# Decoder layer with a product-key expert FFN: three of eight token blocks by gathered rows, gathers two dots early, one-hots scaled on ScalarE

## The reference, cut to what matters

```python
s = jnp.einsum('thpd,hpkd->thpk', q, sub_keys)
s1, i1 = lax.top_k(s[:, :, 0], K); s2, i2 = lax.top_k(s[:, :, 1], K)
cand = (s1[..., :, None] + s2[..., None, :]).reshape(T, H, K * K)
top_s, pos = lax.top_k(cand, K)
idx = jnp.take_along_axis(cand_idx, pos, axis=-1)        # i1 * 128 + i2
g = jax.nn.softmax(top_s, axis=-1)
def block(args):                                          # 128 tokens at a time
    u = jnp.take(u_tab, ib, axis=0)                       # 128 rows of 1024 for each token
    a = jax.nn.gelu(jnp.einsum('cd,ced->ce', xb, u), approximate=False) * gb
    vsel = jnp.take(v_tab, ib, axis=0)
    return jnp.einsum('ce,ced->cd', a, vsel)
```

## Time and profile before

| | us |
|---|---|
| median of 3 runs | 3404.7 (3396.75 to 3407.07) |
| the profiled execution | 3406.95, its span 3405.3 |
| mean granted PE clock of it | 0.951 of 2.4 GHz |
| PE busy | 3045.4 (89%) |
| DVE busy | 2506.8 (74%) |
| POOL busy | 1432.0 (42%) |
| ACT busy | 979.2 (29%) |
| DMA | 695.54 MB, 204 GB/s on average |

### The profile page before, as it was taken

One profiled execution on the slowest core, in us unless ns is written; L12 is line 12 of the kernel. 1 busy time (PEld: TensorE's weight loads), 2 busy tenths in 40 slices (PEclk: granted clock), 3 DMA queues, 4 the chain that ended last, 5 costly groups with the idle time before them and its releaser, 6 DMA issues. The chain is left out here.

```text
span 3405.3 us, 42070 instructions
## 1 busy us (share of the span) xinstructions
PE 3045.4 (89%) x15866; PEld 2729.4 (80%) x15866; DVE 2506.8 (74%) x4479; ACT 979.2 (29%) x1445; POOL 1432.0 (42%) x878
## 2 busy tenths in 40 slices
PE   8996998979998788898888788848999999999997
PEld 6886887869998788898888788847878787878886
DVE  5125773458988877877888776538888888888889
ACT  2113331112222233333333333323333333333331
POOL 4113210006564343343333333336666666656563
PEclk9998999989999998998989899978999999999998
DMA  4214222227775555565555555568787878787882
GB/s 164 99 62 148 91 83 78 76 72 234 247 251 190 184 210 191 203 220 211 178 212 198 188 210 207 212 238 276 278 305 272 294 268 298 273 299 275 281 289 107
DMA packets 294036, 695.54 MB, mean 204 GB/s; under 512 B 20448, under 2 KB 136544, under 8 KB 290656
## 3 DMA queue, kind: packets, MB, share of 16 engines
q1 hardware_dynamic: 190944, 316.66, 28.2%
q0 software_dynamic: 73728, 268.47, 21.8%
q10 hardware_dynamic: 29184, 108.01, 8.2%
HBM read 565.13 MB, written 127.93 MB: 204 GB/s over the span
## 5 line engine op out<-in xcount | busy, mean ns | idle before, releaser
L1066 PE MATMUL z_ps<-hT_hi,u_hi 128*128 128x384 f32 x2048 | 718.6, 351 | 24.1 <-PEq L821 24.1
L794 POOL TENSOR_TENSOR u_lo<-u_raw,u_hi 128x1024 fp32r<-128x1024 f32 x128 | 320.4, 2503 | 994.7 <-ACT u_hi L790 994.5
L1067 PE MATMUL z_ps<-hT_lo,u_hi 128*128 128x384 f32 x2048 | 700.3, 342 | 0.0
L1068 PE MATMUL z_ps<-hT_hi,u_lo 128*128 128x384 f32 x2048 | 698.9, 341 | 0.0
L1357 PE MATMUL y_ps<-v_hi,a_hi 128*128 128x512 f32 x1536 | 603.3, 393 | 65.5 <-DVE a_lo L1458 44.3
L1358 PE MATMUL y_ps<-v_lo,a_hi 128*128 128x512 f32 x1536 | 600.0, 391 | 0.0
L1359 PE MATMUL y_ps<-v_hi,a_lo 128*128 128x512 f32 x1536 | 600.0, 391 | 0.0
L1408 POOL TENSOR_TENSOR v_lo<-room,v_hi 128x1024 fp32r<-128x1024 f32 x128 | 342.2, 2674 | 253.2 <-ACT v_hi L1385 251.5
L1066 PEld LDWEIGHTS z_ps<-hT_hi,u_hi 128*128 128x128 f32 x2048 | 399.3, 195 | 24.7 <-issue 24.2
L1357 PEld LDWEIGHTS y_ps<-v_hi,a_hi 128*128 128x128 f32 x1536 | 289.6, 189 | 139.0 <-DVE a_lo L1458 44.5
L1067 PEld LDWEIGHTS z_ps<-hT_lo,u_hi 128*128 128x128 f32 x2048 | 398.8, 195 | 0.0
(11 more groups left out here) (188 smaller groups left out, 4824.2 us busy)
## 6 DMA issues: line engine op xcount, KB each, us to landing
u_raw<-in_uT SPq DMA_DIRECT2D x128, 512.0 KB
room<-in_v SPq DMA_DIRECT2D x128, 512.0 KB
z<-z_sb ACTq DMA_DIRECT2D x128, 384.0 KB
gates<-g_sb ACTq DMA_DIRECT2D x24, 2048.0 KB
z_in<-z SPq DMA_DIRECT2D x16, 1536.0 KB
g_in<-gates SPq DMA_DIRECT2D x16, 1536.0 KB
room<-z SPq DMA_DIRECT2D x15, 1536.0 KB
room<-gates SPq DMA_DIRECT2D x15, 1536.0 KB
```

Source lines behind the costliest of these rows:

```text
L794: self.nc.gpsimd.tensor_tensor(self.u_lo[e][:], self.u_raw[e][:], self.u_hi[e][:].bitcast(F32), ALU.subtract).then_inc(self.u_lo_in[e], 1)
L1066: nc.tensor.matmul(o, u_hi[e][:, k], hT_hi[:, k, cols], start=(k == 0), stop=False)
L1067: nc.tensor.matmul(o, u_hi[e][:, k], hT_lo[:, k, cols], start=False, stop=False)
L1068: last = nc.tensor.matmul(o, u_lo[e][:, k], hT_hi[:, k, cols], start=False, stop=(k == KT - 1))
```

## The change

Three blocks go by rows and five densely: 384 gathers and dots or additions in each pass where there were 256. z has 640 columns, so the u pass's matmuls have 320 in place of 384, and the v pass has 3840 matmuls in place of 4608. The dots of the u pass are spread unevenly over its turns: 62, 62, 62, 30, 30, 30, 30, 78. Gathers of the u pass are issued two dots ahead of POOL's old place (`EARLY`). The names of the picks are made two heads at a time instead of four. hot1 has two buffers and the multiplication with the gates is four activations with a scale on ACT. h of the third block is loaded once block 0's dots are done.

In the diff SP's program comes first, then PE's, ACT's (`scale_hot` is called in turns from GB on, after z and ahead of `take_gates`), POOL's and DVE's.

```diff
-GB = 2
+GB = 3
-    def names(self, link, half):
+    def names(self, link, two):
-        hs = slice(half * PH // 2, (half + 1) * PH // 2)
+        hs = slice(2 * two, 2 * two + 2)
...
-    RING = 3
-    PER_TURN = GB * PH * TOPK // TB
+    RING, EARLY = 3, 2
+    PER_TURN = [62, 62, 62, 30, 30, 30, 30, 78]
...
+        def own_rows(s, q, n):
+
+            before, k = sum(PER_TURN[:s]), q * 8 + n
+            return range(before + PER_TURN[s] * k // 32, before + PER_TURN[s] * (k + 1) // 32)
...
-                sp.dma_start(h_own[:], d["h"].rearrange("n p c -> p n c")[:, 0:GB]).then_inc(h_here, 16)
+                for b in range(2):
+                    sp.dma_start(h_own[b][:], d["h"][b]).then_inc(h_here[b], 16)
                 for m in range(Q * TB):
+                    done = own_rows(m // Q, m % Q, 0).start // (PH * TOPK)
+                    if done > (own_rows((m - 1) // Q, (m - 1) % Q, 0).start // (PH * TOPK) if m else 0) and done + 1 < GB:
+                        sp.wait_ge(row_used, done * PH * TOPK)
+                        sp.dma_start(h_own[(done + 1) % 2][:], d["h"][done + 1]).then_inc(h_here[(done + 1) % 2], 16)
...
-                    pe.wait_ge(hot_in[g], 4 * gm + n // 2 + 1)
+                    pe.wait_ge(hot_g_in[g], 4 * gm + n // 2 + 1)
...
+                def scale_hot(gm, n):
+
+                    g, t0 = n % 2, gm % Q * GT + 4 * n
+                    act.wait_ge(hot_in[g], 4 * gm + n // 2 + 1)
+                    for t in range(4):
+                        last = nc.scalar.activation(hot1_g[g][:, t], hot1[g][:, t], ACT.Copy,
+                                                    scale=gT[:, t0 + t:t0 + t + 1])
+                    last.then_inc(hot_g_in[g], 1)
...
+                for i in range(EARLY):
+                    gather(i)
...
-                            gather(s * PER_TURN + q * 8 + n)
+                            for i in own_rows(s, q, n):
+                                if i + EARLY < GB * PH * TOPK:
+                                    gather(i + EARLY)
...
-                    elif n == 6 and q % 2:
-                        tk.names(link, q // 2)
+                    elif n == 6:
+                        tk.names(link, q)
...
-                    p = 1 - g
-                    wait(v, hot_in[p], 4 * gm + (n + 1) // 2)
-                    link(nc.vector.tensor_tensor(hot1[:], bc(iota_ps, 1, 4), bc(iT[:, 0, t0:t0 + 4], 2, NK),
-                                                 ALU.is_equal))
-                    nc.vector.tensor_tensor(hot2[g][:], bc(iota_ps, 1, 4), bc(iT[:, 1, t0:t0 + 4], 2, NK), ALU.is_equal)
-                    nc.vector.tensor_tensor(hot1_g[g][:], hot1[:], bc(gT_ps[:, t0:t0 + 4], 2, NK),
-                                            ALU.mult).then_inc(hot_in[g], 1)
+                    for hot, side in ((hot2, 1), (hot1, 0)):
+                        last = nc.vector.tensor_tensor(hot[g][:], bc(iota_ps, 1, 4), bc(iT[:, side, t0:t0 + 4], 2, NK),
+                                                       ALU.is_equal)
+                    last.then_inc(hot_in[g], 1)
...
-                            dot(s * PER_TURN + q * 8 + n)
+                            for i in own_rows(s, q, n):
+                                dot(i)
```

More of the change, by code:

```diff
@@ L711, in __init__ @@
         self.cand, self.cand_left = room.carve(TOPK, TOPK), room.carve(TOPK * TOPK)
-        self.pick = room.carve(2, PH // 2 * TOPK, TOPK)
+        self.pick = room.carve(2, 2 * TOPK, TOPK)
         assert room.taken <= room.LOADED
@@ L716, in __init__ @@
         self.best, self.pos = sb("best", [P, PH, TOPK]), sb("pos", [P, PH, TOPK], U32)
-        self.ab = sb("ab", [P, 2, PH // 2, TOPK], U32)
+        self.ab = sb("ab", [P, 2, 2, TOPK], U32)
         self.gap, self.gap_e = sb("gap", [P, PH, TOPK]), sb("gap_e", [P, PH, TOPK])
@@ L752, in names @@
         link(nc.vector.tensor_tensor(self.pick[:], bc(self.ab[:].rearrange("p a h k -> p a (h k)"), 3, TOPK),
-                                     bc(bc(self.places[:], 1, PH // 2 * TOPK), 1, 2), ALU.is_equal))
+                                     bc(bc(self.places[:], 1, 2 * TOPK), 1, 2), ALU.is_equal))
         for a in range(2):
@@ L969, in _ @@
                 tk.gaps().then_inc(gaps, 1)
-                for half in range(2):
-                    tk.names(link, half)
+                for two in range(PH // 2):
+                    tk.names(link, two)
                 v.wait_ge(exps, 1)
@@ L991, in experts_in @@
         s_in = [sb(f"s_in{j}", [P, 2, NK]) for j in range(2)]
-        iT = sb("iT", [P, 2, P])
+        iT, gT = sb("iT", [P, 2, P]), sb("gT", [P, P])
         hot2 = [sb(f"hot2_{g}", [P, 4, NK]) for g in range(2)]
-        hot1 = sb("hot1", [P, 4, NK])
+        hot1 = [sb(f"hot1_{g}", [P, 4, NK]) for g in range(2)]
         hot1_g = [sb(f"hot1_g{g}", [P, 4, NK]) for g in range(2)]
@@ L997, in experts_in @@
         rows_in = ahead.rows + [sb(f"u_rows{i}", [P, D]) for i in range(RING - len(ahead.rows))]
-        h_own = sb("h_own", [P, GB, D])
+        h_own = [sb(f"h_own{b}", [P, D]) for b in range(2)]
         z_ps = [[bank(f"z_ps{e}{a}") for a in range(2)] for e in range(2)]
@@ L1011, in experts_in @@
         hot_in = [sem(f"hot_in{g}") for g in range(2)]
+        hot_g_in = [sem(f"hot_g_in{g}") for g in range(2)]
         g_done = [sem(f"g_done{g}") for g in range(2)]
@@ L1014, in experts_in @@
         g_stored = [sem(f"g_stored{b}") for b in range(2)]
-        picked_in, h_here = sem("picked_in"), sem("h_own_here")
+        picked_in, h_here = sem("picked_in"), [sem(f"h_own_here{b}") for b in range(2)]
         row_here = [sem(f"u_row_here{i}") for i in range(RING)]
@@ L1141, in _ @@
                             if s >= GB:
+                                scale_hot(gm, n)
                                 if n:
@@ L1184, in _ @@
                 v.wait_ge(const_here, 32)
-                v.wait_ge(h_here, 16)
                 link(nc.vector.tensor_copy(iota_ps, iota[:]))
@@ L1231, in dot @@
                     v.wait_ge(row_here[r], 16 * (i // RING + 1))
+                    if slot == 0:
+                        v.wait_ge(h_here[b % 2], 16 * (b // 2 + 1))
                     wait(v, row_used, i)
-                    nc.vector.tensor_tensor_reduce(rows_in[r][:], rows_in[r][:], h_own[:, b], 1.0, 0.0, ALU.mult, ALU.add,
+                    nc.vector.tensor_tensor_reduce(rows_in[r][:], rows_in[r][:], h_own[b % 2][:], 1.0, 0.0, ALU.mult, ALU.add,
                                                    ahead.z_rows[:, b, slot:slot + 1]).then_inc(row_used, 1)
@@ L1241, in _ @@
                         nc.vector.tensor_copy(iT[:], g_ps[0][:, 0:2])
-                        link(nc.vector.tensor_copy(gT_ps, g_ps[0][:, 2]))
+                        link(nc.vector.tensor_copy(gT[:], g_ps[0][:, 2]))
                     for q in range(Q):
```

## The result

| | before | after |
|---|---|---|
| median (runs) | 3400.7 us (4) | 3594.6 us (4) |
| ratio, with its 95% interval | | 1.057 (1.055 to 1.059) |
| the profiled execution, its span | 3406.95, 3405.3 | 3595.34, 3593.6 |
| mean granted PE clock | 0.951 | 0.885 |

The change makes the kernel 5.7% slower. 3450 us was forecast, with a range of 3310 to 3550.

The account below looks back on a forecast made before the run. PE sets the pace in the v pass and early u turns, DVE close behind; middle u turns wait for gathered rows. 3407 - 51 (u) + 110 (v) - 4 + 2 = 3464, lowered to 3450; range 3310 to 3550.

Parts of the forecast that it names:

- Narrower matmuls: u pass: a matmul of 320 columns repeats every 0.145 us, so a turn's 768 take 111 us instead of 131.
- Turns 0 to 2: u pass, 62 dots each: DVE's work, waits for rows and splits give 195 us a turn, ends 170 and 205.
- Turns 3 to 6: u pass, 30 dots each: row waits go, DVE itself is late next; 160 us a turn, PE's 145 just below.
- Turn 7: u pass, 78 dots: row rate counts, 218 us by three buffers, 210 taken, ends 165 and 230.
- The v turn: v pass: DVE's work, 4.6 us of collisions and rests for rows give 37 us a turn, +110 in all.
- A little under: Whole kernel: 3450 taken instead of the sum 3464, because the two walks lean on latency taken at its high side.
- both walks: Step-by-step walks: a quarter's eight steps in u turns 0 to 2 (15 us a turn lost), and one v turn (37 us).
- both passes bound by DVE's work alone: Rival, u and v passes: 12.4 rows through four buffers with no wait, 3178 to 3230 us; chance 0.07.
- the v pass is milder: Rival, v pass: a turn of 34 us because DMA queues empty in between, 3373 us in all; chance 0.15.
- Rows are there in time: Rival, u pass: rows arrive in time, v pass as forecast, 3318 us in all; chance 0.12.
- Rival 4: u turns 0 to 2: low PE clock makes matmuls 223 us, up to 75 us lost; v turns 39; 3600 us; chance 0.1.
- A page against the rows: Row gathers of 512 KB: the skill's fit gives 3.2 us, the trace 4.84 to 8.4; the forecast sided with the trace.

Follow-up runs that it names:

- g3: Changed kernel with two blocks by rows, 32 dots a turn, four u-pass buffers, gathers three early, step 6's dot moved to step 7: 3216.2 us, 0.943.
- f1: Changed kernel with POOL making only the left half of each v_lo, used twice by PE: 3504.1 us, ratio 1.028.

## Why the prediction was wrong, step by step

The sign and the main mechanism were right: the u pass's narrower matmuls, ACT's scaling and the early gathers return less than the rows of a third block cost, because DVE is behind every row. The sizes were not. The sum of the forecast was 3464; the terms missed by 13 (turns 0 to 2), 41 (turns 3 to 6), 32 (turn 7) and 46 us (the v pass, 152 us longer where 110 - 4 were forecast), together 132: 3596, 1 above the measured time.

- **Narrower matmuls**, estimated at 0.145 us: right. In the trace they start at 1399.67, 1399.81, 1399.96, 1400.11 and 1400.25, 0.145 apart.
- **Turns 0 to 2**, 195 by the sum, 199.2 measured: right. DVE was busy 494.3/3 = 165 us a turn (141 and 20 were taken) and rested 35 (37). One reading in it was off: the surplus of the old dots is 18.7 us a turn by the earlier trace rows, not about 22.
- **Turns 3 to 6**, 160: DVE's busy time was as in the sum (149.8 a turn; 142 and some 7 for meeting the split). The step that failed is "what is late next is DVE itself", with 11 us of rests. It rests 20.7. The difference is the 9.4 us for PE's g_ps, a wait that the walk had no term for: I had taken steps of equal length. At two blocks g3 shows that unequal steps make this wait (14 us a turn, 2.7 with the dot moved); in the changed kernel itself that was not tried. Nor does a run rule out the clock: behind PE's rest of 4.6 us before 1406.37 it was 0.50 from 1407.8 to 1410.1, and the matmuls started 0.27 us apart instead of 0.145. At the 0.94 of these turns that is at most some 10 us of PE's work a turn, an estimate.
- **Turn 7**, 210: the formula 78 x (7 + 1.4)/3 gave 218, and I then took less. (The "54 more rows" beside it are 46; its 66 MB are worked out from 46.) Its round lacked the 1.2 us between a dot's end and the next gather's start, in which POOL is at a split or at the gather before. 1.2 x 26 rounds are 31 us, which brings 218 to 249.
- **The v turn**, 37: the term that failed is the 4.6 us of collisions, carried over unchanged from the kernel before. With half as many row additions again it became 7.6, +3.0. The rests came to 4.3, not 5.5, -1.2. Together 38.8, over 31 turns 56 us more than forecast; the last turn gave 10 back. A guess at why it rises: with eight rows a split meets a row addition less often, and part of DVE's time was a wait for PE. The forecast counted DVE's collisions per turn; per unit of DVE's own work they are 4.6/24.3 = 0.19 and 7.6/26.9 = 0.28, so a rate wouldn't have held either. That the splits are the cause was shown by f1; why the rate rose was not.
- **"A little under"**, -14: there was no row for it, and both walks proved low, not high, so it made the miss larger.

Of the rivals: "both passes bound by DVE's work alone" and "the v pass is milder" (34) fell with 38.8. "Rows are there in time" fell with the rests of turns 0 to 2 (the dots' idle time is 61 + 33 us there) and of turn 7. Rival 4 named a time near the measured one, 3600, but its mechanism isn't seen: in turns 0 to 2 PE was busy for 420.5 of 598.5 us at clock 0.84, so it rested in every turn, and the turns took 199, not 220. The clock did fall, to 0.86 in the v pass, with PE resting 277 us there; the experiments that took away collisions or gathers brought it back to 0.91 and 0.94. In each of them the clock is higher where PE rests less; no run shows it as the cause of a rest, and none held it fixed, so that it costs nothing is argued, not shown.

What was named as proof came as follows. A u pass of 1430 us or so: no, 1521. Rests before dots are gone in turns 3 to 6 and present in 0 to 2 and 7: yes. No wait of PE for ACT's hot_g beyond 1 us a step: on average so in turns 3 to 6 (79.6 us over 128 steps, though in 19 waits of up to 6.4), not in turn 7 (75.3 us over 32 steps). v turn near 37: 38.8. PE well under 98%: yes, 77%. DVE's rest for rows above 5 us a turn: no, 4.3.

**A page against the rows.** The trace decides against the 3.2 us that the forecast set beside its rows. Of turn 7's 78 gathers the fastest twentieth landed in 3.9 us, half in 5.3, the mean is 6.0. By the fit in "DMA: Bandwidth & Descriptors" of the Trainium skill (section on the anatomy of one DMA, SWDGE path), 2.0 us plus bytes/436e3, turn 7 would have been bound by PE and DVE at some 165 us, an estimate; it took 242. Of the pairs of DVE and POOL, the Trainium skill, "SBUF — State Buffer", section "SBUF: two separate sides", says that the engine that comes first holds their shared port for its whole instruction. The timeline agrees that one engine stands for the other's whole instruction: 3.78 us for an addition of 1.27 beside a split of 2.38. It agrees less with who that is. By the starts on record that addition was 0.3 us ahead of the split and still stood. Of the 56 splits of this pass that start during an addition, 34 were held and in 22 the addition was, most of these where the split began 0.3 to 0.5 us behind it.
